# The recurrent mixer's queues on ScalarE and VectorE in another order, and the norms' square root taken earlier, in a two-block transformer forward pass on one core

## What is computed

```python
def odd_mixer(x, w_in, conv_w, conv_b, w_a, b_a, w_x, b_x, lam, w_out):
    gate_branch, xr = jnp.split(x @ w_in, 2, axis=-1)
    xr = causal_dwconv(xr, conv_w, conv_b)
    xb = xr.reshape(bsz, seq, RG_BLOCKS, RG_BLOCK_W)
    r = jax.nn.sigmoid(jnp.einsum('bsnc,ncd->bsnd', xb, w_a).reshape(bsz, seq, D_RNN) + b_a)
    i = jax.nn.sigmoid(jnp.einsum('bsnc,ncd->bsnd', xb, w_x).reshape(bsz, seq, D_RNN) + b_x)
    log_a = (-LRU_C * r.astype(jnp.float32)) * jax.nn.softplus(-lam.astype(jnp.float32))
    a = jnp.exp(log_a)
    u = jnp.sqrt(-jnp.expm1(2.0 * log_a)) * (i * xr).astype(jnp.float32)
    _, h = lax.associative_scan(lru_combine, (a, u), axis=1)
    y = h.astype(x.dtype) * jax.nn.gelu(gate_branch)
    return y @ w_out
```

## Time and profile before

| | |
|---|---|
| median of 3 runs | 1967.78 us |
| the profiled execution, as a run | 1967.11 us |
| its span, first to last instruction | 1965.3 us |
| TensorE busy | 1884.1 us, 96% |
| VectorE busy | 1351.2 us, 69% |
| ScalarE busy | 937.6 us, 48% |
| mean granted TensorE clock | 0.970 of full speed |

### The profile page before, as it was taken

The page is one execution under the profiler, slowest core; times in us unless marked ns, Lnnn a source line. Parts: engine busy times, 40 slices in busy tenths (PEclk is TensorE's granted clock), DMA queues, the critical chain, the costliest instruction groups (busy, mean ns, idle before and its releaser), DMA issues.

```text
span 1965.3 us, 34117 instructions
## 1 busy us (share of the span) xinstructions
PE 1884.1 (96%) x14532; PEld 1825.0 (93%) x14532; DVE 1351.2 (69%) x1676; ACT 937.6 (48%) x1101; POOL 134.5 (7%) x119
## 2 busy tenths in 40 slices
PE   7969999988999999999999999999999999999997
PEld 7938999988999899989999999989998999999997
DVE  5797898566799656666785666656665686576664
ACT  5443665446666444444354454435443444354442
POOL 0000333000132100000300000000000030000000
PEclk9968999998999999999999989999999999989999
DMA  7312555533455534554455445554555445445451
GB/s 283 141 43 76 179 197 185 201 119 129 172 196 191 199 142 175 192 193 156 168 199 188 172 150 178 189 212 145 177 190 205 144 177 191 166 150 193 179 206 67
DMA packets 46797, 334.82 MB, mean 170 GB/s; under 512 B 5184, under 2 KB 5568, under 8 KB 6464
## 3 DMA queue, kind: packets, MB, share of 16 engines
q1 hardware_dynamic: 46512, 332.20, 47.0%
q0 software_dynamic: 144, 0.52, 0.1%
HBM read 331.65 MB, written 1.05 MB: 169 GB/s over the span
## 4 chain that ended last, share of the span: by engine, by line
PE 89%; DVE 7%; ACT 2%; issue 1%; DMA 1%; SPq 0%; DVEq 0%; ACTq 0%
PE psum L240 20%; PE psum L241 19%; PE psum L242 19%; PE psum L255 10%; PE psum L277 8%; PE psum L258 5%; PE psum L284 3%; DVE w_lo L222 2%; PE psum L316 1%; DVE scratch L1262 1%; PE psum L483 1%; PE psum L486 1%; PE psum L485 1%; PE psum L338 1%; DMA w_raw<-stream_in 0%
## 5 line engine op out<-in xcount | busy, mean ns | idle before, releaser
L213 ACT ACTIVATE w_hi<-w_raw 128x2048 fp32r<-128x2048 f32 x313 | 598.1, 1914 | 764.9 <-PE psum L242 457.9
L240 PE MATMUL psum<-x_split,w_hi 128*128 128x256 f32 x2984 | 848.1, 284 | 11.0 <-DVE x_split L354 10.4
L241 PE MATMUL psum<-x_split,w_hi 128*128 128x256 f32 x2984 | 845.1, 283 | 0.0
L242 PE MATMUL psum<-x_split,w_lo 128*128 128x256 f32 x2984 | 845.0, 283 | 0.0
L222 DVE TENSOR_TENSOR w_lo<-w_raw,w_hi 128x2048 fp32r<-128x2048 f32 x313 | 717.4, 2296 | 69.1 <-ACT w_hi L213 69.1
L240 PEld LDWEIGHTS psum<-x_split,w_hi 128*128 128x128 f32 x2984 | 573.5, 192 | 12.3 <-issue 11.2
L241 PEld LDWEIGHTS psum<-x_split,w_hi 128*128 128x128 f32 x2984 | 573.6, 192 | 0.1
L242 PEld LDWEIGHTS psum<-x_split,w_lo 128*128 128x128 f32 x2984 | 573.4, 192 | 0.0
L296 DVE TENSOR_TENSOR scratch<-psum,inv_rms 128x512 f32<-128x512 f32 (+1 forms) x205 | 139.5, 687 | 254.2 <-PE psum L242 238.7
L255 PE MATMUL psum<-h_split,w_hi 128*128 128x512 f32 x816 | 288.6, 399 | 0.0
L258 PE MATMUL psum<-h_split,w_lo 128*128 128x256 f32 x816 | 229.2, 281 | 0.0
(11 more groups left out here) (203 smaller groups left out, 1900.4 us busy)
## 6 DMA issues: line engine op xcount, KB each, us to landing
w_raw<-stream_in SPq DMA_DIRECT2D x313, 1024.0 KB, 4.8
x_resid<-x_in SPq DMA_DIRECT2D x1, 1024.0 KB, 6.9
y_out<-x_resid SPq DMA_DIRECT2D x4, 256.0 KB, 2.5
scratch<-mask_in SPq DMA_DIRECT2D x1, 768.0 KB, 11.0
scratch<-ev_in SPq DMA_DIRECT2D x1, 512.0 KB, 9.6
scratch<-inv_in POOLq DMA_DIRECT2D x1, 512.0 KB, 3.9
params<-par_in SPq DMA_DIRECT2D x1, 247.0 KB, 7.2
matrices<-mat_in SPq DMA_DIRECT2D x1, 192.0 KB, 9.0
```

Of the source, the lines that this page charges most:

```text
L213: act.activation(w_hi[:, n % RING, :], raw[:, n % RAWS, :], ACT.Copy).then_inc(hi_ready, 1)
L240: pe.matmul(dst, w_hi[:, c.slot, b:b + P], src[:, k0 + k, 0, :], start=opens, stop=False)
L241: pe.matmul(dst, w_hi[:, c.slot, b:b + P], src[:, k0 + k, 1, :], start=False, stop=False)
L242: done = pe.matmul(dst, w_lo[:, c.slot, b:b + P], src[:, k0 + k, 0, :], start=False, stop=last and k == nk - 1 and m == len(tiles_) - 1)
```

## The change

- ScalarE takes the recurrent mixer's work in the order in which TensorE produces it: both first groups' last taps together, the sigmoid table loaded by a dummy operation, gelu 0 no longer ahead of the sigmoids but with gelu 1 after the square roots, the high part of group 3 between sigmoids 1 and 2, each refill ahead of the work that follows it.
- VectorE makes the low part of a group behind the next group's eviction; the evictions of the gate chunks, the refills and the products y0 and y1 stand in other places.
- In all nine norms at a stage's start, the recurrent mixer's included, the mean's matmuls stand behind inner step 0 and the spreading behind step 4 (one hunk for all); the square root stands ahead of the refills in ScalarE's queue, the copy of the spread root between them, and the reciprocal ahead of VectorE's refill.

The arithmetic of each value is the same. Definitions that only move into functions, and the lists of names, are left out here.

```diff
@@ -367,7 +367,7 @@
                     pe.wait_ge(pair_taken, c.event + 1)
                     pe.wait_ge(lo_ready, c.number + 1)
                     multiply(pe, c, pair_tiles(c.bank), xs, 0, KT, True, True, signal=(chunk_done, 1),
-                             hooks={3: lambda: mean_pe(pe, tr, summed, l), 6: lambda: rinv_pe(pe, tr, l)})
+                             hooks={0: lambda: mean_pe(pe, tr, summed, l), 4: lambda: rinv_pe(pe, tr, l)})
                     done = 3
                 whole_pe(pe, ph, n, l, done)
 
@@ -628,13 +628,13 @@
             for c in chunks(phase, n, l):
                 at = c.n
                 act.wait_ge(chunk_done, c.number + 1)
-                refill_hi(act, c)
                 if at == 0:
                     chunk0 = c
+                    rms_act(act, pre, l)
+                    refill_hi(act, c)
+                    rinv_act(act, pre, l)
                     continue
-                if at == 1:
-                    rms_act(act, pre, l)
-                    rinv_act(act, pre, l)
+                refill_hi(act, c)
                 if conv:
                     if at == 1:
                         taps(chunk0)
@@ -691,8 +691,8 @@
                     refill_lo(dve, c)
                     continue
                 if at == 1:
+                    inverse_dve(dve, pre, l)
                     refill_lo(dve, c)
-                    inverse_dve(dve, pre, l)
                     dve.wait_ge(*pre["stat"].after("copied", l))
                     take_scaled(dve, chunk0, S(PRE + 2 * chunk0.slot, 2))
                     take_scaled(dve, c, S(PRE + 2 * c.slot, 2))
...
-            for g in G4:
-                c = Chunk("od_xr", g)
-                act.wait_ge(chunk_done, c.number + 1)
-                refill_hi(act, c)
-                if g == 0:
-                    continue
-                if g == 1:
-                    rms_act(act, N["mixnorm1"], 0)
-                    rinv_act(act, N["mixnorm1"], 0)
-                    xr_rest(0)
-                xr_rest(g)
...
-            c = Chunk("od_gate0", 0)
-            act.wait_ge(chunk_done, c.number + 1)
-            refill_hi(act, c)
-            gelu(c, 0)
-            for j in range(8):
+
+            def sigmoids(j):
                 q, s = divmod(j, 4)
-                c = Chunk("od_ax", q)
                 if s == 3:
-                    act.wait_ge(chunk_done, c.number + 1)
+                    act.wait_ge(chunk_done, Chunk("od_ax", q).number + 1)
                 else:
...
-                if j == 3:
-                    refill_hi(act, c)
...
+            act.wait_ge(chunk_done, xr[0].number + 1)
+            rms_act(act, N["mixnorm1"], 0)
+            refill_hi(act, xr[0])
+            rinv_act(act, N["mixnorm1"], 0)
+            act.wait_ge(chunk_done, xr[1].number + 1)
+            refill_hi(act, xr[1])
+            last_tap(0)
+            last_tap(1)
+            xr_high(0)
+            act.wait_ge(chunk_done, xr[2].number + 1)
+            refill_hi(act, xr[2])
+            xr_high(1)
+            last_tap(2)
+            act.wait_ge(chunk_done, xr[3].number + 1)
+            refill_hi(act, xr[3])
+            xr_high(2)
+            last_tap(3)
+            act.activation(small[:, 6:7], eps, ACT.Sigmoid)
+            act.wait_ge(chunk_done, gate0.number + 1)
+            refill_hi(act, gate0)
+            sigmoids(0)
+            sigmoids(1)
+            xr_high(3)
+            sigmoids(2)
+            sigmoids(3)
+            refill_hi(act, Chunk("od_ax", 0))
+            for j in range(4, 8):
+                sigmoids(j)
+            refill_hi(act, Chunk("od_ax", 1))
...
-            refill_hi(act, c)
-            gate = [Chunk("od_gate", g) for g in range(3)]
             act.wait_ge(chunk_done, gate[0].number + 1)
+            refill_hi(act, gate[0])
+            gelu(gate0, 0)
             gelu(gate[0], 1)
             high(0)
-            refill_hi(act, gate[0])
+            act.wait_ge(chunk_done, gate[1].number + 1)
+            refill_hi(act, gate[1])
             high(1)
-            act.wait_ge(chunk_done, gate[1].number + 1)
             gelu(gate[1], 2)
-            refill_hi(act, gate[1])
             high(2)
-            act.wait_ge(chunk_done, gate[2].number + 1)
             gelu(gate[2], 3)
             high(3)
+            act.wait_ge(chunk_done, gate[2].number + 1)
             refill_hi(act, gate[2])
...
+                if g == 0:
+                    rms_act(act, N["normM"], l)
                 refill_hi(act, c)
-                if g == 1:
-                    rms_act(act, N["normM"], l)
+                if g == 0:
                     rinv_act(act, N["normM"], l)
...
-            for g in G4:
-                c = Chunk("od_xr", g)
-                if g == 0:
-                    chunk0 = c
-                    refill_lo(dve, c)
-                    continue
-                if g == 1:
-                    refill_lo(dve, c)
-                    inverse_dve(dve, N["mixnorm1"], 0)
-                    dve.wait_ge(*N["mixnorm1"]["stat"].after("copied"))
-                    take_scaled(dve, chunk0, S(TMP + 2 * chunk0.slot, 2))
-                take_scaled(dve, c, S(TMP + 2 * c.slot, 2))
-                if g > 1:
-                    refill_lo(dve, c)
-                if g == 1:
-                    xr_rest(0)
-                xr_rest(g)
-            c = Chunk("od_gate0", 0)
-            take_scaled(dve, c, S(GB, 2))
-            refill_lo(dve, c)
+
+            refill_lo(dve, xr[0])
+            inverse_dve(dve, N["mixnorm1"], 0)
+            refill_lo(dve, xr[1])
+            dve.wait_ge(*N["mixnorm1"]["stat"].after("copied"))
+            branch(0)
+            branch(1)
+            conv(0)
+            conv(1)
+            xr_low(0)
+            branch(2)
+            refill_lo(dve, xr[2])
+            xr_low(1)
+            conv(2)
+            branch(3)
+            refill_lo(dve, xr[3])
+            xr_low(2)
+            conv(3)
+            take_scaled(dve, gate0, S(GB, 2))
+            xr_low(3)
+            refill_lo(dve, gate0)
...
-            for j in range(8):
-                q, s = divmod(j, 4)
-                c = Chunk("od_ax", q)
-                if j == 3:
-                    refill_lo(dve, c)
-                if j:
-                    decay(j - 1)
-            decay(7)
+            for j in range(4):
+                decay(j)
+            refill_lo(dve, Chunk("od_ax", 0))
+            for j in range(4, 8):
+                decay(j)
+            refill_lo(dve, Chunk("od_ax", 1))
...
                 if h == 0:
-                    refill_lo(dve, c)
-            gate = [Chunk("od_gate", g) for g in range(3)]
+                    take_scaled(dve, gate[0], S(GB + 2, 2))
+                    refill_lo(dve, gate[0])
...
-            take_scaled(dve, gate[0], S(GB + 2, 2))
             scan(0)
+            take_scaled(dve, gate[1], S(GB + 4, 2))
+            scan(1)
+            refill_lo(dve, gate[1])
             gated(0)
-            scan(1)
-            refill_lo(dve, gate[0])
+            gated(1)
             lo(0)
-            gated(1)
-            take_scaled(dve, gate[1], S(GB + 4, 2))
             scan(2)
             lo(1)
             gated(2)
-            refill_lo(dve, gate[1])
             scan(3)
             take_scaled(dve, gate[2], S(GB + 6, 2))
...
                 if g == 1:
+                    inverse_dve(dve, N["normM"], l)
                     refill_lo(dve, c)
-                    inverse_dve(dve, N["normM"], l)
                     dve.wait_ge(*N["normM"]["stat"].after("copied", l))
```

More of the change, by code:

```diff
@@ L993, in odd_act, with last_tap, xr_high @@
             A = od_act
-            def xr_rest(g):
-                c = Chunk("od_xr", g)
-                act.wait_ge(*taken(c.event))
+            xr = [Chunk("od_xr", g) for g in G4]
+            gate0 = Chunk("od_gate0", 0)
+            gate = [Chunk("od_gate", g) for g in range(3)]
+            def last_tap(g):
+                act.wait_ge(*taken(xr[g].event))
                 for t, nm in enumerate("ab"):
                     k = 2 * g + t
-                    act.activation(S1(XC + k), S1(TMP + 2 * c.slot + t), ACT.Identity,
+                    act.activation(S1(XC + k), S1(TMP + 2 * xr[g].slot + t), ACT.Identity,
                                    scale=par1[:, PAR1["odw"] + 4 * k + 3:PAR1["odw"] + 4 * k + 4],
                                    bias=par1[:, PAR1["odb"] + k:PAR1["odb"] + k + 1]).then_inc(*A.did(f"{nm}_{g}"))
+            def xr_high(g):
                 act.wait_ge(*od_dve.after(f"b3_{g}"))
@@ L1005, in xr_rest @@
                    .then_inc(*A.did(f"hi{g}"))
[L1006 to L1016 removed]
+            def sigmoids(j):
+                q, s = divmod(j, 4)
+                if s == 3:
+                    act.wait_ge(chunk_done, Chunk("od_ax", q).number + 1)
+                else:
+                    act.wait_ge(ax_done, 3 * q + s + 1)
```

(14 more changed lines are left out.)

25 lines of the change are left out of this document (9 added, 16 removed).

## The result

The kernel after has a median of 1953.36 us over 4 runs (1953.15 to 1953.52), the kernel before, run beside it, 1967.62 us over 4 (1966.84 to 1968.02). The ratio is 0.9928 with a 95% interval of 0.9913 to 0.9944: 14.3 us faster by the medians, 13.7 us by the two profiled executions (1967.11 and 1953.41), where 12.9 had been forecast.

A forecast was written before the change was run, and what follows sets the result against it. TensorE bounds the kernel; only its idle time and low clock in the recurrent mixer, at most 22.8 us, could be won. od_out's first eviction moves from S+93.0 to S+80.1, 12.9 us: 1967.11 becomes 1954.2, range 1951.5 to 1959.0.

The forecast's parts named there:

- Start: Start of the recurrent mixer: the root comes sooner but the first eviction does not, S+18.8 against S+18.5 before.
- S: Zero point of the mixer's times: the start of od_xr's first pair of chunks, 397.17 in the profile before.
- First stop: TensorE's wait for step 0's sigmoid in od_ax: 1.0 us instead of 9.67 + 0.9, with no low clock after it.
- Second stop: TensorE's wait before od_out: it starts at S+65.8 after 5.6 us of standing, where it was S+79.1.
- Restart: TensorE's 48 matmuls of od_out's steps 0 to 5 take 8.5 us, 5.5 us of them at the low clock.
- Level: At od_out, TensorE's 48 matmuls end at S+74.3, just when y3's high part is done.
- Rival (a): TensorE, not y3, bounds od_out: low clock through all 48 matmuls, 11.5 us; gain 10.0, 1957.8 us; chance 0.13.
- Other stages: The same norm moves outside the recurrent mixer save nothing: taken as 0, bounds -0.5 and +1.5 us over all.
- Rival (b): The mixer's new queue stands longer than counted, each wait going 1:1 to the end; with 3 to 4 us, 1958.5; chance 0.12.
- (c): Load into chunk 60's freed slot lands sooner or isn't waited for: 1.6 us sooner there, gain 15, 1952.8 us; chance 0.10.

The follow-up runs named there:

- the rounding later: Kernel after with ScalarE's rounding of chunk 63 behind the first exp, tanh and square, not ahead of their table load: median 1951.06 us, ratio 0.9922.
- the kernel after without the norm part: Kernel after with the reordering of mean, spreading, root and reciprocal taken back in all nine norms at a stage's start: median 1952.26 us, ratio 0.9924.
- a table load more: Kernel after with a dummy sigmoid between the exponentials and the four square roots, so one more ScalarE table load: median 1955.19 us, ratio 0.9931.
- w_lo of chunk 64 late: Kernel after with VectorE's w_lo of chunk 64 behind y2 and ahead of the last scans, not ahead of y0: median 1957.34 us, ratio 0.9952.
- low parts last: Kernel after with VectorE's low parts of y0 to y2 behind y3, and the last eviction ahead of the last scans: median 1951.37 us, ratio 0.9927.

## Why the prediction was right

- **What bounds it.** Right: the gain is where TensorE stood still. Of the 18.2 us idle in the mixer some 8.5 are left (2.2, 5.65 and 0.66), and of 9.2 us of work at the low clock 4.1, which gives back half of the difference, 2.5. These 9.7 and 2.5 make up the 12.1 us of the mixer.
- **Start.** First eviction S+18.8 forecast, S+19.15 measured.
- **First stop.** Forecast 1.0, measured 2.2; the clock stayed at 1.00 behind it, as said. The sigmoids start at S+37.1, 0.8 late: 0.35 from the start and the rest on the way through the convolution. TensorE was also some 0.2 us sooner at the stop than counted. That the clock stayed up was in part luck (see the last section).
- **Second stop.** w_lo of chunk 60 done at S+42.1 (forecast 41.2), load landed S+47.2 (46.2), the interval 5.0 as counted; roots from S+58.1, y0's high part lets TensorE start at S+66.8 (65.8) after 5.65 us idle (5.6), y3's high part done at S+75.0 (74.3), od_out's first eviction S+80.9 (80.1). So the whole shortfall of the mixer's sum, 12.1 for 12.9, is already there at the w_lo of chunk 60: the term that was too small is VectorE's way through the convolution, 23.0 us for 22.4 counted, and the start.
- **Restart.** TensorE's 48 matmuls took S+66.8 to S+74.4, 7.6 us for 8.5: the low clock lasted 4.1 us of work for 5.5 assumed. It then waited 0.66 us for y3. "Level" was right within 1 us, and which of the two comes last depends on the execution too: in the run with the rounding later the low clock lasted 6.0 us, the 48 took 8.5 us (463.23 to 471.73), and TensorE came last. Rival (a), the low clock through all 48, is in none of the profiles.
- **Other stages.** 0 fits what the runs show of the norm part, but for a reason that isn't complete: TensorE stood at no root at a stage's start in the profile of before, and did at four in that of the kernel after without the norm part. The 1.6 us that the two profiled executions differ by there were counted by nobody. They go with the execution and not with the change, so part of the nearness of 13.7 and 14.3 us to the 12.9 forecast is luck: the mixer alone gives 12.1.
- **Rival (b)** had the right slope on the line over the convolution, the exponentials and the roots (3.5, 3.7 and 1.34 us for 3.4, 3.7 and 1.50) but not at the first stop itself: TensorE 0.74 us sooner through it won 0.08. **(c)** didn't occur; the load was waited for, and its price was right (1.6 worked out, 1.78 measured).
- **Wrong in its reason:** "Only 9.5 of it is the earlier sigmoid; the rest is that TensorE no longer restarts" splits the gain as if the parts added up. 5.7 us of earlier sigmoid gave 3.5, and 1.9 of it gave minus 1.0, as long as gelu 0 held up y0 and the w_lo of chunk 64 stood late. Taken back singly the parts cost 3.5, 3.7 and 4.8 us, 12.0 in all; added singly one of them cost time.

## What to carry to other kernels

With two stops one behind the other, follow the line that ends at the second one back to its start before you price the first: here 0.74 us won at the first stop, off that line, was worth 0.08 at the end. Moving one instruction in one queue can be worth nothing, as gelu 0 was, until the queue that waits for it is moved too, so judge a reordering as a whole and by taking single parts back from it. And where executions differ by some microseconds, compare the length of the stage in the profiles, not the medians.

## What was not expected of the hardware

- An execution's low-clock stretches differ with the same code: at the same place of the program behind the mixer 10.20 us in the profile of the run with a table load more and 6.80 in that of the kernel after, and 10.22 in that of before. By the estimate above that is worth 1.0 us. The rest of the kernel took 1460.4 to 1463.5 us in the fourteen profiles.
- A stop of 2.30 us was followed by full clock up to od_out in three of the five profiles that have it (the kernel after, w_lo of chunk 64 late, rounding of 63 later), and by a stretch at the low clock in two (a table load more, low parts last), although all five have the same program up to there. The window of the last one behind the stop:

```profile
434.35:437.60 3.25, 3.25 (x20) 3.25 (x21) 2.56 (x3) 3.25 (x8) 0.00 (x0) 0.69 0.41 169
```

  TensorE reached od_out 1.5 us later in these two, at S+62.5 and not S+61.05, and the second stop covered it. So the prediction's step that so short a stop takes no clock held for the profiled execution of the kernel after and not for every one.
